# A hybrid mLSTM and sparse-attention layer: x handed over columns-first, bias tables from the host, the first weight pair in halves, unread products at the start, two transposes moved

## The reference

```python
h = _rmsnorm(x, norm_gain)
proj = h @ w_in                     # 4096 -> 15416 columns
(m_q, m_k, m_v, m_o, m_z, m_i, m_f, a_q, ck, cv, sk, sv, wk, wv, a_gate, a_z) = \
    jnp.split(proj, split_points, axis=-1)
...
h_m = _mlstm(mq, mk, mv, i_pre, f_pre)          # 4 heads, gated, normalised -> y_m
o_a = _nsa(a_q, ck, cv, sk, sv, wk, wv, a_gate, # 16 heads in 4 groups
           cmp_k_pos, cmp_k_w1, cmp_k_w2, cmp_v_pos, cmp_v_w1, cmp_v_w2, rel_bias)
...
mix = jnp.concatenate([y_m, y_a], axis=-1).astype(x.dtype)
x = x + mix @ w_out                 # 4096 x 4096
return _rmsnorm(x, final_norm_gain)
```

## Time and profile before

| | |
|---|---|
| device time, median of 3 runs | 1859.42 us (1858.14 to 1859.46) |
| span of the profiled execution, first to last instruction | 1852.8 us |
| median minus span (what lies around the span) | 6.6 us |
| PE busy | 1824.5 us, 98% of the span |
| DVE, ACT, POOL busy | 1140.7, 828.6, 77.1 us |
| DMA | 345.66 MB, mean 187 GB/s |
| block 0, first matmul to the first of block 1 | 9.72 to 69.52 us |

### The profile page before, as it was taken

The page is one execution under the profiler, slowest core; times in us unless marked ns, Lnnn a source line. Parts: engine busy times, 40 slices in busy tenths (PEclk is TensorE's granted clock), DMA queues, the critical chain, the costliest instruction groups (busy, mean ns, idle before and its releaser), DMA issues.

```text
span 1852.8 us, 24286 instructions
## 1 busy us (share of the span) xinstructions
PE 1824.5 (98%) x8488; PEld 1514.5 (82%) x8488; DVE 1140.7 (62%) x1461; ACT 828.6 (45%) x1120; POOL 77.1 (4%) x54
## 2 busy tenths in 40 slices
PE   8989999999999999999999999999999999999997
PEld 6878888888888888888888888888888888888886
DVE  5534554467677676777666666756675775555554
ACT  5534544445444544544444444444444544444443
POOL 0000000000101010010000000000000000000000
PEclk9989999999999999999999999999999999999999
DMA  8676666654656555456666666666666667666664
GB/s 268 185 189 198 197 191 193 193 165 144 181 147 174 153 160 169 147 160 175 191 194 191 172 193 194 188 175 193 194 190 173 178 214 236 205 205 203 206 205 174
DMA packets 210543, 345.66 MB, mean 187 GB/s; under 512 B 20340, under 2 KB 65908, under 8 KB 210324
## 3 DMA queue, kind: packets, MB, share of 16 engines
q1 hardware_dynamic: 203720, 332.68, 60.5%
q10 hardware_dynamic: 6736, 11.77, 2.6%
HBM read 337.07 MB, written 7.33 MB: 186 GB/s over the span
## 4 chain that ended last, share of the span: by engine, by line
PE 95%; DMA 2%; DVE 1%; ACT 1%; issue 1%; POOL 0%; DVEq 0%; ACTq 0%; POOLq 0%; SPq 0%
PE acc_a L509 15%; PE acc_a L511 15%; PE acc_a L510 15%; PE acc_b L509 14%; PE acc_b L511 14%; PE acc_b L510 14%; DMA w_raw<-in_w_in 2%; PE bank_v L516 1%; ACT w_split L911 1%; PE bank_z L757 1%; PE bank_x L511 1%; PE bank_x L510 1%; PE bank_x L509 0%; DVE w_split L1274 0%; PE bank_v L517 0%
## 5 line engine op out<-in xcount | busy, mean ns | idle before, releaser
L1274 DVE TENSOR_TENSOR w_split<-w_raw,w_split 128x1024 fp32r<-128x1024 f32 x620 | 776.8, 1255 | 602.8 <-ACT w_split L911 599.7
L911 ACT ACTIVATE w_split<-w_raw 128x1024 fp32r<-128x1024 f32 x620 | 655.2, 1059 | 857.4 <-PE acc_a L511 418.9
L509 PE MATMUL acc_a<-w_split,lhs_hi 128*128 128x512 f32 x1216 | 484.3, 398 | 2.3 <-DVE lhs_lo L1343 2.2
L509 PE MATMUL acc_b<-w_split,lhs_hi 128*128 128x512 f32 x1216 | 479.5, 394 | 0.4 <-issue 0.4
L511 PE MATMUL acc_a<-w_split,lhs_lo 128*128 128x512 f32 x1216 | 475.7, 391 | 0.0
L510 PE MATMUL acc_a<-w_split,lhs_hi 128*128 128x512 f32 x1216 | 475.4, 391 | 0.0
L511 PE MATMUL acc_b<-w_split,lhs_lo 128*128 128x512 f32 x1216 | 473.7, 390 | 0.0
L510 PE MATMUL acc_b<-w_split,lhs_hi 128*128 128x512 f32 x1216 | 473.6, 389 | 0.0
L511 PEld LDWEIGHTS acc_a<-w_split,lhs_lo 128*128 128x128 f32 x1216 | 229.2, 189 | 49.0
L509 PEld LDWEIGHTS acc_a<-w_split,lhs_hi 128*128 128x128 f32 x1216 | 229.5, 189 | 48.5 <-issue 2.5
L511 PEld LDWEIGHTS acc_b<-w_split,lhs_lo 128*128 128x128 f32 x1216 | 228.3, 188 | 48.2
(11 more groups left out here) (274 smaller groups left out, 929.8 us busy)
## 6 DMA issues: line engine op xcount, KB each, us to landing
w_raw<-in_w_in SPq DMA_DIRECT2D x416, 512.0 KB
w_raw<-in_w_out SPq DMA_DIRECT2D x128, 512.0 KB
w_raw<-in_w_in SPq DMA_DIRECT2D x128, 256.0 KB
wide<-in_x SPq DMA_DIRECT2D x8, 512.0 KB, 10.0
xres<-in_x ACTq DMA_DIRECT2D x8, 512.0 KB, 4.2
out_y<-wide SPq DMA_DIRECT2D x8, 512.0 KB, 3.3
toe_dram<-toe_row ACTq DMA_DIRECT2D x4, 766.0 KB, 10.3
toe<-toe_dram ACTq DMA_DIRECT2D x4, 512.0 KB, 4.4
```

The costliest lines, as they stand in the source:

```text
L509: pe.matmul(dst, a[0], b[0], start=start, stop=False)
L911: act.activation(w_hi[:, cols], w_raw[:, cols], ACT.Copy).then_inc(hi_done, 1)
L1274: dve.tensor_tensor(w_lo[:, cols], w_raw[:, cols], w_hi[:, cols].bitcast(F32), ALU.subtract).then_inc(lo_done, 1)
```

## The change

The host now also hands over x transposed (`x_cols_first`, 128 rows of 32 x 256 values), the gains as 128x32, one table of constants of 128x1318 (identity, masks, positions, convolution weights, the compressed blocks' bias) and the key bias as 128x4096 (`toe_bias`).

- Block 0 has no transposes of x, no `prepare_rows`, no `prepare_bias`. ACT and DVE make `lhs_hi` and `lhs_lo` from `x_t` in SBUF, which shares its space with `lhs_lo`. SP loads `x_t` in seven pieces among the weight pairs 0 to 7, and x in its natural layout, which the norm and nothing else in this block needs, among pairs 8 to 15. ACT's eight squarings stand behind slots 8 to 15.
- `copies_out` and the table in DRAM are gone; each group's bias is one load.
- The first weight pair is loaded and split in two halves, and PE starts when the first half's high part is there.
- Before that PE runs eight 128x512 products of a tile of ones into bank v that nothing reads.
- The transposes `T_CK` move from behind pair 0 of block 1 to behind pair 5, `T_CV` from before block 2 to behind its first pair, `T_SK` from behind pair 0 of block 3 to behind pair 1.

```diff
+            fetch_xt(0)
+            sp.dma_start(slot_of(0, 0, 1), w_in[0:P, C_KV:C_KV + BW]).then_inc(half_in, 16)
+            sp.dma_start(slot_of(0, 1, 1), w_in[P:2 * P, C_KV:C_KV + BW]
+                         ).then_inc(w_loaded[0], LOADED)
+            fetch_xt(1)
             columns(0, C_KV, [1])
+            fetch_xt(2)
+            columns(0, C_KV, [2, 3])
+            fetch_xt(3)
+            fetch_xt(4)
+            columns(0, C_KV, [4])
+            fetch_xt(5)
+            columns(0, C_KV, [5, 6])
+            fetch_xt(6)
+            columns(0, C_KV, [7])
+            for i in range(8):
+                columns(0, C_KV, [8 + i])
                 fetch_x(i)
...
+            pe.wait_ge(warm_set, 1)
+            for _ in range(WARM):
+                pe.matmul(bv[:, :], warm[:, 0:P], warm[:, :], start=True, stop=True)
...
-            for c in range(PAIRS):
+            first_pair()
+            for c in range(1, PAIRS):
                 pe.wait_ge(ht_lo, c + 1)
                 pair(0, c, 0)
-                if c + 2 < PAIRS:
-                    x_t(c + 2)
-                if c == 6:
-                    prepare_rows()
-                if c in (8, 9):
-                    prepare_bias(c - 8)
-            pe.wait_ge(pre_dve, 2)
-            pe.wait_ge(pre_act, 2)
-            stream(1, 1, {1: [lambda: transpose_stage(T_CK, 0)]})
+            pe.wait_ge(consts_in, 16)
+            stream(1, 1, {6: [lambda: transpose_stage(T_CK, 0)]})
...
-            transpose_stage(T_CV, 1)
...
+                if c == 1:
+                    transpose_stage(T_CV, 1)
...
-            stream(3, 1, {1: [key_block], 2: [hidden_t], 7: [compressed, running_sum],
+            stream(3, 1, {2: [key_block, hidden_t], 7: [compressed, running_sum],
...
+            act.dma_start(gain_t[:, :], gains).then_inc(gain_in, 16)
+            act.dma_start(c128[:, :], consts).then_inc(consts_in, 16)
...
             for c in range(PAIRS):
-                if c + 2 < PAIRS:
-                    x_hi(c + 2)
+                if c + 3 < PAIRS:
+                    first_hi(c + 3)
                 slot(0, c)
...
-                if c % 2 == 1:
-                    t, i = divmod(c // 2, 4)
+                if c >= PAIRS - 8:
+                    i, t = divmod(c - (PAIRS - 8), 2)
                     act.wait_ge(x_in[2 * i], 16)
                     act.wait_ge(x_in[2 * i + 1], 16)
                     link(act.activation(junk[:, :], x_nat[:, t, i * 1024:(i + 1) * 1024],
                                         ACT.Square, accum_out=ss8[:, t, i:i + 1]))
```

More of the change, by code:

```diff
@@ L574, in prepare_rows @@
[L574 to L578, removed]
-                pe.transpose(bx[:, 192:192 + KT_IN // 2], gain_m_rows[:, :],
-                             ident[0:KT_IN // 2, 0:KT_IN // 2])
-                for c in range(16):
-                    last = pe.transpose(bx[:, 128 + 4 * c:132 + 4 * c],
-                                        conv_rows[:, c * P:(c + 1) * P], ident[0:4, 0:4])
-                last.then_inc(pre_pe, 1)
-                pe.matmul(by[0:HEADS_A, 0:TOE], rb[:, :], hot_down, start=True,
-                          stop=True).then_inc(pre_pe, 1)
@@ L602, in _, with first_pair @@
-            x_t(0)
-            x_t(1)
-            pe.wait_ge(pre_act, 1)
-            for c in range(PAIRS):
+            pe.wait_ge(warm_set, 1)
+            for _ in range(WARM):
+                pe.matmul(bv[:, :], warm[:, 0:P], warm[:, :], start=True, stop=True)
+            def first_pair():
+                for k in range(2):
+                    w = [m[:, k * BW:(k + 1) * BW] for m in (w_hi, w_lo)]
+                    a = [[m[:, k, t * P:(t + 1) * P] for m in (lhs_hi, lhs_lo)] for t in range(TT)]
+                    if k == 0:
+                        pe.wait_ge(ht_hi, 1)
+                        pe.wait_ge(half_hi, 1)
+                    else:
+                        pe.wait_ge(hi_done, 1)
+                    for t in range(TT):
+                        pe.matmul(acc[0][t][:, :], a[t][0], w[0], start=k == 0, stop=False)
+                    if k == 0:
+                        pe.wait_ge(ht_lo, 1)
+                    for t in range(TT):
+                        pe.matmul(acc[0][t][:, :], a[t][1], w[0], start=False, stop=False)
+                    if k == 0:
+                        pe.wait_ge(half_lo, 1)
+                    else:
+                        pe.wait_ge(lo_done, 1)
+                    for t in range(TT):
+                        last = pe.matmul(acc[0][t][:, :], a[t][0], w[1], start=False, stop=False)
+                last.then_inc(pe_used, 1)
@@ L1337, in _, with first_lo, mix_lo @@
             dve.memset(ones[:, :], 1.0)
-            def x_lo(c, gain=gain_t, banks=acc[1]):
+            def first_lo(c):
                 dve.wait_ge(ht_hi, c + 1)
+                for kk in (2 * c, 2 * c + 1):
+                    last = dve.scalar_tensor_tensor(
+                        lhs_lo[:, kk, :], x_t[:, kk, :], gain_t[:, kk:kk + 1],
+                        lhs_hi[:, kk, :].bitcast(F32), ALU.mult, ALU.subtract)
+                last.then_inc(ht_lo, 1)
+            def mix_lo(c):
+                dve.wait_ge(ht_hi, PAIRS + c + 1)
@@ L1392, in positions_lo @@
                 last.then_inc(pre_dve, 1)
-            stream(1, {2: [lambda: transposed(T_CK, *two(cin[0], by_group))],
-                       6: [positions_lo]})
+            stream(1, {7: [lambda: transposed(T_CK, *two(cin[0], by_group))],
+                       11: [positions_lo]})
             dve.wait_ge(tr_done, T_CK + 1)
```

340 lines of the change are left out of this document (137 added, 203 removed).

## The result

The changed kernel is **slower**, by 0.6%: 1868.37 us, median of 4 runs (1867.47 to 1868.75), against 1858.78 us (4 runs, 1856.73 to 1859.46) of the kernel before on the same chip. The ratio is 1.0059, 95% interval [1.0046, 1.0071]. The forecast was 1832.5 us, so 36 us are missing. The profiled execution of it took 1868.21 us with a span of 1866.4: 1.8 us lie around the span.

The account below looks back on a forecast made before the run. PE, busy for 98% of the span, was taken to bound the kernel. From the median 1859.42 us, 15.5 + 0.2 + 9.8 + 1.4 = 26.9 us were subtracted, giving 1832.5 us, range 1829.2 to 1837.2.

Parts of the forecast that it names:

- 2.73 us a pair: PE's time for one weight pair's products, taken from block 1 of the kernel before and used for block 0 after.
- D: Rival: reading x columns-first goes slowly, as the table's copies did, making the kernel slower; 1866 us at 0.09 MB/us; chance 0.01.
- first product: Start of block 0: PE starts its first real product at 6.9 us instead of 9.72.
- wait at pair 5: Block 0: PE reaches pair 5 at 22.9 us and waits half a microsecond for its loads, starting at 23.45.
- block 0 saved: Without transposes of x, block 0 is limited by loads and ends at 54.0 instead of 69.5 us: 15.5 us saved.
- landing rule: Loads in block 0 land at 3.2 us + bytes at 0.39 MB/us, to 0.4 us, fitted on the kernel before.
- added half microsecond for ACT's lack of slack: Block 0, slots 8 to 12: ACT needs about 3.15 us against PE's 2.73, so its end moves from 53.5 to 54.0.
- rival B: The start is starved: loads after pair 0 run at 0.34 instead of 0.39 MB/us, 4.1 us less saved, 1836.6; chance 0.13.
- The unread products: Eight products before block 0's first real one: cost nothing, no gain counted from an earlier clock rise, at most 2.4 us.
- The stall of block 1: PE's wait ahead of block 2 goes with the table copies: 5.75 us idle plus 4.05 us of lower clock, 9.8 saved.
- The moved transposes: T_CK in block 1 saves 0.2 us, T_SK in block 3 saves 1.4; T_CV's wait is within the 9.8 us term.
- 6.6 us around the span: Difference between median 1859.42 and span 1852.8; held untouched by the change, so span savings are subtracted from the median.

Follow-up runs that it names:

- experiment 1: The changed kernel with the space for lhs_lo and x_t reserved without the 8 extra columns (32 bytes): 1827.22 us, ratio 0.9839 to the kernel before.
- experiment 2: The kernel before with 32 unused bytes ahead of w_raw, so that w_raw, w_split and the scratch space move: 1897.34 us, ratio 1.0217.
- experiment 3: The kernel before with 32 unused bytes ahead of w_split and 32 more behind it: 1897.73 us, ratio 1.021.
- experiment 5: The kernel before with 32 unused bytes ahead of lhs_hi, so that both operands of the products move alike: 1857.06 us, ratio 1.000.
- the aligned kernel: The changed kernel without the 32 extra bytes behind lhs_lo and x_t: 1827.22 us, ratio 0.9839 to the kernel before.
- experiment 10: The aligned kernel with an early start (no unread products, a tiny activation first, constants asked for inside block 0): 1826.47 us.
- experiment 11: The aligned kernel with only the first group of transposes (T_CK) put back behind pair 0 of block 1: 1830.57 us.
- experiment 12: The aligned kernel run again unchanged, on the same chip as experiment 10 and experiment 11: 1826.86 us.
- experiment 7: The aligned kernel with all three groups of transposes back at their old places: 1835.36 us.
- experiment 9: The kernel before with only the key bias taken from the host, so no copies into a table in DRAM: 1846.15 us, ratio 0.9944.

## Why the prediction was wrong

**The step that failed** is one that the sum never names: that the products which the change does not touch keep their pace. The prediction takes 2.73 us a pair from block 1 of the kernel before and uses it for block 0 of the kernel after, and in the other blocks it lets the difference of pace be nothing. The opening sentence gives three ways in which PE's time line can shrink (fewer matmuls, less idle time, the higher clock); a fourth, the distance from matmul to matmul at an unchanged clock, was left out, and it moved by 2.6%, from 227.2 to 233.2 ns, which is 41 us in the time. The `+ 8` was in the changed kernel to be read. Experiments 1, 2, 3 and 5 show the cause at full size, in both directions: 41 us off the kernel after when the 32 bytes go, 40 to 41 us on the kernel before when they come to `w_split` alone, nothing when both operands move. Of the rivals none had it, and D, the one on the slow side, was false: the windows show reads of `x_t` and weights together at 402 GB/s.

**The terms themselves** can be read in the aligned kernel's trace, against the trace before:

| step | forecast | measured |
|---|---|---|
| first product | 6.9 | 6.63 |
| pair 1 ready | 11.35 | 11.64 (kernel after; in the aligned one PE is the later) |
| wait at pair 5 | 0.55 at 22.9 | 0.64, ends at 23.2 |
| block 0 saved | 15.5 (block 1 at 54.0) | 16.2 (53.27) |
| from there to block 3's transposes: 0.2 + 9.8 + 1.4 | 11.4 | 11.6 = (199.34 - 69.52) - (174.19 - 53.27) + 2.73 for the extra pair |
| behind them | 0 | 0.3 |
| sum of spans | 26.9 | 28.1 |
| sum of medians | 26.9 | 29.9 |

So with the pace put right the parts hold, but the time does not quite: 1827.2 us is 5.3 below the forecast and 2.0 below its range. 3.0 of it are more saved than forecast; 2.3 are the starting value, 1859.42 from three runs against 1857.13 from nine.

Block 0 was right, with its mechanism: DMA sets the pace, and the landing rule gave the split of pair 1 (forecast 9.0, measured 8.94) and the wait at pair 5. The first product's time was right to 0.3 us partly by luck. The sum had ACT wait for the first half of the weights until 6.3 us. It was on hand by 5.85, since the split starts there without a wait, and what stood between the arrival of x and it was the load of ACT's table, 1.28 us, and x's high part, 0.9 us (experiments 10 to 12), terms that the sum doesn't have on this path. The added half microsecond for ACT's lack of slack in slots 8 to 12 was hardly needed: block 1 starts at 53.27 and 53.63 in the two profiles of the aligned kernel, where the forecast without it was 53.5. The prediction's 2.8 us for the first 12 matmuls at the lower clock should be 12 x 0.2 = 2.4; the sum doesn't use it. The loads kept 397 GB/s from 20 to 28 us, so rival B's 332 belonged to the old order of transfers. The Trainium skill, page "DMA: Bandwidth & Descriptors", section Specifications, gives a limit of about 358 GB/s for a core. The trace disagrees again: 402 GB/s over 16 us.

**The clock at the start.** The unread products were priced at nothing, and are. In the kernel after, the first pair ran at the higher clock (starts 0.23 us apart), in the aligned one at the lower (0.43 us apart) until about 11 us, while the windows list 1.00 for both. This is no effect of the 32 bytes: with the same list at the start, the profile of experiment 11 has the higher clock there and those of 7 and 12 the lower; why is open. It makes little difference in the end, since PE then waited 1.98 us for pair 1 in the kernel after and not at all in the aligned one, as the prediction said of this gain.

**The stall of block 1** was 9.8 forecast, 8.5 measured by experiment 9 and 0.96 more by the moved transposes, 9.5 together. Medians show more (10.1 for experiment 9 alone) because the stall and the stretch at the lower clock behind it differ from run to run. In the profile of experiment 5, which runs the same lists as the kernel before, the wait and a window behind it are

```profile
PE bank_v L559 <- issue: 8.5, 1, 8.5
```

```profile
126.00:142.00 16.00, 16.00 (x52) 13.71 (x52) 2.52 (x4) 3.08 (x4) 0.00 (x0) 0.50 0.23 50
```

against 5.6 in the earlier trace rows and a clock that is back at 1.00 from 128.3 us on, in an execution of 1863.4 us. The waits in experiments 2 and 3 are 7.9 and 6.8 us, and the lower clock lasts 10.2 us in the profile before and 6.8, 17.1 and 23.9 us in those of experiments 2, 3 and 5. With the stall gone the times also lie closer: 1845.54 to 1846.44 us in experiment 9, against 1853.87 to 1859.13 of the kernel before on the same chip. That also mends the forecast's "6.6 us around the span": 1.8 to 1.9 us lie around it in every profiled execution with both numbers. By that the profiled execution before took about 1854.7 us (an estimate, 1852.8 + 1.9), less than each of the four timed runs, 1856.73 to 1859.46. So a part of the gain was not in the rows at all.

**The moved transposes** are three groups (the title says two). For the first group the prediction took 0.2 us. As a difference to the kernel before that is right, but what the move is worth in the new kernel is 3.7 us: without it the shorter block 0 would have made a new wait of 2.8 us with a fall of the clock. The prediction named this cover (five pairs, 13.7 us) without pricing its absence. The third group's wait of 1.4 us came out to the digit in experiment 7. Of the 8.1 us that all three are worth, the waits are 5.2; the stretch at the lower clock, 3.4 us in the windows of experiment 7, explains 1.7 more, and 1.2 us stay unexplained.

## What to carry to other kernels

Before predicting a change to a matmul-bound kernel, compare where the operands lie as well as what the lists do: any buffer that grows moves everything allocated behind it. Here the pace was best when the start of the moving operand minus that of the stationary one was a multiple of 256 bytes; the 2.6% it costs otherwise is spread over all products, shows in no wait and in no clock, and here it hid a gain of 1.6%. Two numbers show it: the mean duration of one unchanged group before and after, and the start-to-start distance in a quiet stretch.

The best of the kernels run is the aligned one with the early start, 1826.47 us, ratio 0.9838 [0.9825, 0.9852] to the kernel before; the aligned kernel alone, one line away from the change, has nearly all of that.

## What the runs showed of the hardware

- 512-column float32r matmuls follow each other at 226.7 ns when the two operands' starts in SBUF are a multiple of 256 bytes apart, and at 228.7 to 236.6 ns at the other distances tried. Moving both by the same 32 bytes changes nothing, and it is the same with all other engines and DMA idle. Only the distances in the table and this one shape were tried; why it is so is open. The Trainium skill, page "TensorE: Matmul & The Clock Gate", section "Wait — 56ns, not 53.3ns?", gives 215.7 ns for 512 columns at the higher clock; no series here was that fast.
- After a change of offsets a series at a distance of 0 or 256 needed 6 to 11 products at 224 to 236 ns before its pace was even, but none from (256,0) to (512,0) and one from (0,128) to (0,256).
- The same lists ran with 6.8 to 23.9 us at the lower clock behind the stall of 5.6 to 8.5 us ahead of block 2 (the kernel before and experiments 2, 3 and 5).
- A load of ACT's table took 1.28 us, and stood behind the first wait of the list where the first activation stood. The Trainium skill, page "ScalarE: Activation LUTs", section "What ACT_TABLE_LOAD costs", gives about 1283 ns for the load; the trace agrees. It adds some 1380 ns of drain for a switch of sets; here the first activation follows 0.01 us behind the load.
